# Memory keys and values as plain fp32 products, and a buffer of its own for the early weight tile of a stage

## The chip, the cores and the metric

The kernel runs on one core of a Trainium2 chip. The metric is the device time of one launch in microseconds (us), the median of several runs. Before the change three runs took 1684.59, 1685.55 and 1691.52 us.

## The reference

The program computes two transformer blocks of two layers each on a sequence of 256 tokens, width 1024, all in float32. Block 1 has a sliding-window attention with sinks and a sparse attention that keeps the 64 best keys of an index score; block 2 has a latent attention (MLA), a compressed/selected/window attention (NSA), a cross-attention to 256 memory tokens and a feed-forward net with a short convolution. The change touches the keys and values of the memory and the places where a weight tile is fetched early:

```python
memn = layer_norm_2(mem, ln_mem_g, ln_mem_b)                # once
for l in range(DEPTH):                                      # block 2, each layer
    ...                                                     # MLA and NSA, output projection, norm 1
    q = (x @ wq).reshape(B, S, XA_HEADS, XA_DH)             # XA_HEADS 4, XA_DH 256
    k, v = jnp.split(memn @ wkv, 2, axis=-1)                # wkv: 1024 x 2048
    s = jnp.einsum('bshd,bmhd->bhsm', q, k) * (XA_DH ** -0.5)
    o = jnp.einsum('bhsm,bmhd->bshd', jax.nn.softmax(s, -1), v)
    x = layer_norm_2(DEEPNORM_ALPHA * x + o @ wo, ln2_g, ln2_b)
```

`memn @ wkv` does not depend on the layers before it, so it can be computed at any time.

## The kernel before

Nearly every weight matrix comes as tiles of one megabyte (128 partitions x 2048 floats, line 653, issued by the sync engine SP). They land in a ring of five buffers, `raw`. Each is then split in two: ScalarE (ACT) writes the rounded high half `whi` (line 1171, three buffers), VectorE (DVE) subtracts it from the raw values to get the low half `wlo` (line 1498, five buffers). The activations are split in the same way (`xhi`, `xlo`; `memhi`, `memlo` for the memory). A product (`product`, lines 687 to 689) is then three matmuls in the fast reduced-precision fp32r format: high with high, high with low, low with high. `serve(key)` issues all splits whose high buffer is free once the tile of `key` is done on TensorE (PE); `hi_room` and `raw_room` give the tile that has to be done first. TensorE counts its finished tiles in `tile_done`.

Some products are plain fp32 matmuls on unsplit data: the attention scores and values, the compression weights `w1` (line 1063), and in the cross-attention the scores (line 1135) and values (line 1153). In the record of a run such a matmul leaves two entries: line 1135 runs 2 x 4 x 2 = 16 times a layer, 32 in all, and there are 64 entries.

The memory's keys and values of one layer of block 2 are eight tiles, `("kv", l, k)`. Four are worked off during each of the four attentions of the program (block 1 layers 0 and 1, block 2 layers 0 and 1). A tile is two halves (`memory_half`, line 766), each of 8 steps over the width, so 24 fp32r matmuls of 256 columns; there are 4 x 8 = 32 halves. `memory_slot` says at which attention step a half stands: steps 0 to 6 and 8 in block 1, steps 0, 2, 4, 6, 8, 10, 11 and 12 in block 2. ScalarE copies a half out (`memory_store`, line 1239) and sends it to memory.

An attention is a software pipeline over steps (a unit of a head kind and 128 tokens, in two halves of the heads). In step i TensorE does scores(i), a memory half, values(i-3), transposes(i-2). VectorE does the mask and the maximum of step i (line 1586), in block 1 also a piece of the top-k search (`top`), then the normalization of step i-1 (line 1620) and, behind some steps, a split. ScalarE does the exponentials of step i (line 1259), the copy of the memory half, and the copies of transposed probabilities (line 1282). Every engine works in the order in which its program was written.

Ahead of the attention in block 1, during the input projection, VectorE applies the rotary embedding (lines 1564 to 1569) and sums the index scores (line 1779) for token halves 0 and 1; the rectified scores that it sums come from ScalarE (line 1327) after TensorE (line 915).

Nine tiles are "extra" (`plan_extra`): the first tile of a stage behind an attention or a norm (`pg`, `xq`, `g` and `in`, each with index 0). They have no place in the ring. Their raw data land in the second half of `sy`, their halves in `ext`. The first half and second half of `sy` also hold the attention's probabilities (`soft`), so the load of `pg` 0 waits for the last values product of the attention (`pv_done`), that of `xq` 0 stands on SP behind the same wait, and that of `g` 0 in block 2 waits for the cross-attention (`xpT_ready`). In `split_order` an extra tile stands ahead of the ring tile it is tied to: `pg` 0 ahead of `o` 3, `xq` 0 ahead of `out` 3.

The output projection (`o` in block 1, `out` in block 2, four tiles) runs on TensorE in the order: tile 0 for both token halves, then tiles 1, 2, 3 for token half 0, then 1, 2, 3 for token half 1.

## Time and profile before

| | |
|---|---|
| median of three runs | 1685.55 us |
| the profiled execution | 1690.54 us, of which the recorded span is 1688.5 us |
| TensorE busy | 1534.9 us, 91% of the span |
| VectorE busy | 1097.6 us, 65% |
| ScalarE busy | 745.8 us, 44% |
| mean granted TensorE clock | 0.949 of full speed |
| the 217 low-half splits on VectorE | 489.6 us |
| the 217 high-half splits on ScalarE | 410.0 us |

The profile records one execution. PE is matmuls, DVE VectorE, ACT ScalarE, SP the sync engine that issues loads. An idle engine costs only where something waits for it. A matmul's recorded length is longer than its share of the array, since matmuls overlap in a pipeline: what one costs is read from start to start. The granted clock is a share of full speed, and its two levels are 2.4 GHz (1.0) and 1.2 GHz (0.5).

### The profile page before, as it was taken

What the parts mean: (1) busy time and instruction counts of PE and PEld (TensorE: products, weight loads), DVE (VectorE), ACT (ScalarE), POOL (GpSimd) and SP (SyncE); (2) the same over time, 40 slices, a digit from 0 to 9 for tenths busy, and PEclk for the clock granted to TensorE, in tenths of its full rate; (3) what the DMA queues carried; (4) which work ended last, traced back from release to release, by engine and by line L of the source; (5) the groups of instructions that cost most, each with busy time, mean ns of one, the idle gap of its engine ahead of it and who ended that gap; (6) DMA issues with size and microseconds to landing.
All of it is one profiled execution on the core that took longest, in us unless ns stands there. A gap on an engine that the chain in (4) does not pass through costs nothing.

```text
span 1688.5 us, 24734 instructions
## 1 busy us (share of the span) xinstructions
PE 1534.9 (91%) x10037; PEld 1380.7 (82%) x10037; DVE 1097.6 (65%) x1696; ACT 745.8 (44%) x1058; POOL 65.3 (4%) x58
## 2 busy tenths in 40 slices
PE   6788999999879999989888898999998888989997
PEld 5676899998767999968877778999788767789996
DVE  6886965467977754575464556677754745566766
ACT  4454433334553433334564334454445633344542
POOL 1200000000100000011000000000010000000000
PEclk9989999999899999989799999999997999989998
DMA  8523555655324655644424634556444246345551
GB/s 295 173 80 105 193 189 185 206 191 180 104 81 168 208 209 187 224 138 123 148 67 134 200 106 153 191 181 219 150 128 143 66 134 200 111 153 187 184 191 50
DMA packets 184692, 267.29 MB, mean 158 GB/s; under 512 B 7382, under 2 KB 139396, under 8 KB 184452
## 3 DMA queue, kind: packets, MB, share of 16 engines
q1 hardware_dynamic: 179684, 260.48, 46.6%
q10 hardware_dynamic: 4896, 5.25, 0.9%
q8 instruction: 80, 1.31, 0.3%
q14 instruction: 32, 0.26, 0.1%
HBM read 260.46 MB, written 5.24 MB: 157 GB/s over the span
## 4 chain that ended last, share of the span: by engine, by line
PE 66%; DVE 17%; DVEq 5%; ACT 4%; issue 3%; DMA 2%; POOL 2%; SPq 0%; ACTq 0%; POOLq 0%
PE psw L687 15%; PE psw L688 14%; PE psw L689 14%; PE psa L687 5%; PE psa L688 5%; PE psa L689 5%; DVE wlo L1498 4%; POOL rstd L2129 2%; DVE sy L1586 1%; DVE xtok L1530 1%; DVE r L1884 1%; PE psw L800 1%; DVEq L1590 1%; PE psa L822 1%; PE psw L1063 1%
## 5 line engine op out<-in xcount | busy, mean ns | idle before, releaser
L1498 DVE TENSOR_TENSOR wlo<-raw,whi 128x2048 fp32r<-128x2048 f32 (+2 forms) x217 | 489.6, 2262 | 299.3 <-ACT whi L1171 298.8
L1171 ACT ACTIVATE whi<-raw 128x2048 fp32r<-128x2048 f32 (+2 forms) x217 | 410.0, 1891 | 335.5 <-PE psw L689 243.4
L687 PE MATMUL psw<-xhi,whi 128*128 128x256 f32 x1472 | 416.8, 283 | 2.3 <-ACT r L1358 1.4
L688 PE MATMUL psw<-xlo,whi 128*128 128x256 f32 x1472 | 416.5, 283 | 0.0
L689 PE MATMUL psw<-xhi,wlo 128*128 128x256 f32 x1472 | 416.5, 283 | 0.0
L687 PEld LDWEIGHTS psw<-xhi,whi 128*128 128x128 f32 x1472 | 282.4, 192 | 4.7 <-ACT r L1358 2.2
L688 PEld LDWEIGHTS psw<-xlo,whi 128*128 128x128 f32 x1472 | 282.4, 192 | 1.2
L689 PEld LDWEIGHTS psw<-xhi,wlo 128*128 128x128 f32 x1472 | 282.5, 192 | 0.0
L687 PE MATMUL psw<-whi,xhi 128*128 128x512 f32 (+3 forms) x472 | 186.7, 396 | 28.6 <-DVE wlo L1498 26.1
L688 PE MATMUL psw<-wlo,xhi 128*128 128x512 f32 (+3 forms) x472 | 183.0, 388 | 0.0
L689 PE MATMUL psw<-whi,xlo 128*128 128x512 f32 (+3 forms) x472 | 182.2, 386 | 0.0
L687 PE MATMUL psa<-whi,rr 128*128 128x512 f32 x352 | 139.1, 395 | 5.4 <-DVE wlo L1498 5.4
L688 PE MATMUL psa<-wlo,rr 128*128 128x512 f32 x352 | 138.4, 393 | 0.0
L687 PEld LDWEIGHTS psw<-whi,xhi 128*128 128x128 f32 x472 | 91.3, 193 | 48.8 <-DVE wlo L1498 29.6
L689 PE MATMUL psa<-whi,rr 128*128 128x512 f32 x320 | 124.5, 389 | 0.0
L1471 ACT ACTIVATE r<-psw,pcol 128x256 f32<-128x256 f32 x88 | 45.0, 562 | 145.9 <-PE psw L689 145.9
L2084 DVE SCALAR_TENSOR_TENSOR r<-psw,pcol,r 128x255 f32<-128x255 f32 (+1 forms) x176 | 72.7, 475 | 54.2 <-ACT r L1471 52.6
L689 PEld LDWEIGHTS psw<-whi,xlo 128*128 128x128 f32 x472 | 91.5, 194 | 16.9
L688 PEld LDWEIGHTS psw<-wlo,xhi 128*128 128x128 f32 x472 | 91.5, 194 | 15.5
L2129 POOL TENSOR_TENSOR rstd<-vare,mhalf 128x1 f32<-128x1 f32 x26 | 39.6, 1524 | 1497.0 <-DVE vare L1520 1497.0
L1259 ACT ACTIVATE sy<-sy,nmx 128x256 f32<-128x256 f32 (+1 forms) x160 | 70.6, 444 | 45.9 <-DVE nmx L1599 45.9
L687 PEld LDWEIGHTS psa<-whi,rr 128*128 128x128 f32 x352 | 67.0, 190 | 19.2 <-issue 6.2
(270 smaller groups left out, 2147.0 us busy)
## 6 DMA issues: line engine op xcount, KB each, us to landing
raw<-in_w_gu SPq DMA_DIRECT2D x44, 1024.0 KB, 5.1
raw<-in_ffn_w_up SPq DMA_DIRECT2D x42, 1024.0 KB, 5.1
raw<-in_w_down SPq DMA_DIRECT2D x22, 1024.0 KB, 4.9
raw<-in_ffn_w_down SPq DMA_DIRECT2D x22, 1024.0 KB, 5.0
raw<-in_w_in SPq DMA_DIRECT2D x20, 1024.0 KB, 5.4
raw<-in_xa_wkv SPq DMA_DIRECT2D x16, 1024.0 KB, 5.7
raw<-in_w_o SPq DMA_DIRECT2D x8, 1024.0 KB, 5.1
raw<-in_w_out SPq DMA_DIRECT2D x8, 1024.0 KB, 5.1
```

The source lines that it names most:

```text
L687: pe.matmul(o, lh, rh, start=first, stop=False)
L688: pe.matmul(o, lh, rl, start=False, stop=False)
L689: return pe.matmul(o, ll, rh, start=False, stop=last)
L800: ins = pe.matmul(psw[:, 2 * (i % 2) + a, b * S:b * S + nk], qT(kind, h, t), kT(kind, h, nk), start=True, stop=True)
L822: ins = pe.matmul(psa[64 * b:64 * b + DH, 2, (h // 2) * P:(h // 2 + 1) * P], v(kind, h, kb), pt[:, m % 4, (q % 4) * P:(q % 4 + 1) * P], st ...
L1063: ins = pe.matmul(psw[:, i, 0:2 * NC], w1[:, j, :], cf[i][:, j, :, :].rearrange("p g n -> p (g n)"), start=(j == 0), stop=(j == 15))
L1171: nc.scalar.activation(tile_flat("hi", i), tile_flat("raw", i), ACT.Copy).then_inc(hi_ready, 1)
L1259: ins = nc.scalar.activation(soft[:, u % 2, h, 0:nk], soft[:, u % 2, h, 0:nk], ACT.Exp, bias=nmx[:, u % 2, h:h + 1], scale=1.0, accum_out= ...
L1471: ins = nc.scalar.activation(buf[:, f % 2, ch, :], bank2(psw, bank)[:, ch, :], ACT.Identity, scale=pcol[:, 2 + 2 * l, cc:cc + 1], bias=pco ...
L1498: v.tensor_tensor(tile_flat("lo", i), tile_flat("raw", i), tile_flat("hi", i).bitcast(F32), ALU.subtract).then_inc(lo_ready, 1)
L2084: ins = v.scalar_tensor_tensor(out=o, in0=bank2(psw, bank)[:, ch, 0:S - lag], scalar=pcol[:, j, cc:cc + 1], in1=o, op0=ALU.mult, op1=ALU.add)
L2129: g.tensor_tensor(rstd[:, t:t + 1], vare[:, t:t + 1], mhalf[:, t:t + 1], ALU.pow).then_inc(ln_rstd, 1)
```

## The change

The 16 `kv` tiles are no longer split: TensorE multiplies the raw tile with the unsplit transposed memory `memT`, one plain fp32 matmul a step in place of three fp32r ones. The 16 high-half and 16 low-half splits go, and the four low halves of the memory. A buffer of its own, `xraw`, takes the raw data of the extra tiles; their loads wait only until the previous extra tile is done. Outside the `in` stages an extra tile is now split behind its ring tile. The norm parameters ahead of `xq` are loaded two tiles later in SP's order. The wait for the stored memory halves moves with them.

```diff
-    halved = [i for i in ring if tiles[i][0][1] != "w1"]
+    halved = [i for i in ring if tiles[i][0][1] not in ("w1", "kv")]
@@
-        split_order += [e for e in extra if extra[e] == i] + [i]
+        here = [e for e in extra if extra[e] == i]
+        split_order += here + [i] if here and tiles[here[0]][0][1] == "in" else [i] + here
@@
-        memhi = sb("memhi", [KD, S], F32R)
-        memlo = sb("memlo", [KD, S], F32R)
+        memT = sb("memT", [KD, S])
+        xraw = sb("xraw", [2048])
@@
-                return {"raw": sy[:, 1, :], "lo": ext[:, 1, :], "hi": ext[:, 0, :]}[buf]
+                return {"raw": xraw[:], "lo": ext[:, 1, :], "hi": ext[:, 0, :]}[buf]
@@
-            gb_before[ti[(2, "xq", l, 0)]] = (2, "1", l)
+            gb_before[ti[(2, "xq", l, 2)]] = (2, "1", l)
@@
-                if key[1] == "xq" and key[3] == 0:
+                if key[1] == "xq" and key[3] == 2:
@@
-                if key[1] == "pg" and i in extra:
-                    sp.wait_ge(pv_done, 2 * (unit0(1, key[2]) + 4))
-                elif key[1] == "g" and i in extra:
-                    sp.wait_ge(xpT_ready, 4 * (key[2] + 1))
+                if i in extra and extra_use[i]:
+                    sp.wait_ge(tile_done, max(e for e in extra if e < i) + 1)
@@ memory_half
-                if half == 0:
-                    wh, wl = take(key)
-                else:
-                    wh, wl = tile_view("hi", ti[key]), tile_view("lo", ti[key])
+                pe.wait_ge(*loaded(ti[key]))
@@
-                        ins = product(psa[:, 3, 0:TC], wh[:, k, piece], wl[:, k, piece], memhi[:, k, :],
-                                      memlo[:, k, :], k == 0, k == KD - 1)
+                        ins = pe.matmul(psa[:, 3, 0:TC], weight[:, k, piece], memT[:, k, :],
+                                        start=k == 0, stop=k == KD - 1)
@@ ScalarE, input projection of block 1, layer 0
-                            turned_hi((2, "mem", 0), t, memhi)
+                            for b in range(2):
+                                act.wait_ge(mem_turned, 2 * t + b + 1)
+                                nc.scalar.activation(memT[:, 4 * b:4 * b + 4, t * P:(t + 1) * P], turned_bank(t, b),
+                                                     ACT.Copy).then_inc(mem_ready, 1)
@@ VectorE, the same place
-                    if l == 0 and q == 2:
-                        for t in range(NT):
-                            turned_lo((2, "mem", 0), t, memhi, memlo)
```

The order of VectorE's work ahead of the second layer's attention in block 1, before (`r` is its scratch, `sy` the rectified scores and temporaries):

```order
L1498 TENSOR_TENSOR wlo<-raw,whi 128x2048 [waits hi_ready] x2
L1564 TENSOR_TENSOR sy<-r,cos 128x576 [waits proj_ready]
...
L1498 TENSOR_TENSOR wlo<-raw,whi 128x2048 [waits hi_ready]
L1779 SCALAR_TENSOR_TENSOR r<-sy,wi_s,causal 128x128 [waits relu_done]
L1779 SCALAR_TENSOR_TENSOR r<-sy,wi_s,r 128x128 x7
L1564 TENSOR_TENSOR sy<-r,cos 128x640 [waits proj_ready]
...
L1498 TENSOR_TENSOR wlo<-raw,whi 128x2048 [waits hi_ready]
L1779 SCALAR_TENSOR_TENSOR r<-sy,wi_s,causal 128x256 [waits relu_done]
```

And now, on the same engine at the same place (line numbers are those of the changed kernel):

```order
L1499 TENSOR_TENSOR wlo<-raw,whi 128x2048 [waits hi_ready]
L1565 TENSOR_TENSOR sy<-r,cos 128x576 [waits proj_ready]
...
L1780 SCALAR_TENSOR_TENSOR r<-sy,wi_s,causal 128x128 [waits relu_done]
L1780 SCALAR_TENSOR_TENSOR r<-sy,wi_s,r 128x128 x7
L1565 TENSOR_TENSOR sy<-r,cos 128x640 [waits proj_ready]
...
L1780 SCALAR_TENSOR_TENSOR r<-sy,wi_s,causal 128x256 [waits relu_done]
```

Three splits are gone from between the rotary embedding and the index sums.

ScalarE at the end of the first attention of block 2, before: the extra tile `xq` 0 (`ext`) ahead of `out` 3 (the `whi` behind it), then `xq` 1.

```order
L1282 ACTIVATE pt<-psa 128x512 [waits pv_done,pt_done] x2
L1271 ACTIVATE xhi<-psa 128x4x128 [waits pv_done]
L1171 ACTIVATE ext<-sy 128x2048 [waits extra_loaded]
L1171 ACTIVATE whi<-raw 128x2048 [waits tile_done,tile_loaded2]
L1171 ACTIVATE whi<-raw 128x2048 [waits tile_done,tile_loaded3]
```

And now:

```order
L1280 ACTIVATE pt<-psa 128x512 [waits pv_done,pt_done] x2
L1269 ACTIVATE xhi<-psa 128x4x128 [waits pv_done]
L1169 ACTIVATE whi<-raw 128x2048 [waits tile_done,tile_loaded2]
L1169 ACTIVATE ext<-xraw 128x2048 [waits extra_loaded]
L1169 ACTIVATE whi<-raw 128x2048 [waits tile_done,tile_loaded3]
```

The split of `out` 3 has moved ahead of the extra one, which reads another buffer. VectorE's low halves moved in the same way.

SP at the same place, before (`gb` are the norm's parameters):

```order
L653 DMA raw<-in_w_out 128x4x512 [waits tile_done] x4
L615 DMA gb<-in_ln_g 128x1024 [waits kv_stored1,x_ready,kv_stored0,pv_done]
L616 DMA gb<-in_ln_b 128x1024
L653 DMA sy<-in_xa_wq 128x8x256
L653 DMA raw<-in_xa_wq 128x8x256 [waits tile_done] x3
```

And now:

```order
L654 DMA raw<-in_w_out 128x4x512 [waits tile_done] x4
L654 DMA xraw<-in_xa_wq 128x8x256 [waits tile_done]
L654 DMA raw<-in_xa_wq 128x8x256 [waits tile_done]
L618 DMA gb<-in_ln_g 128x1024 [waits kv_stored1,x_ready,kv_stored0,pv_done]
L619 DMA gb<-in_ln_b 128x1024
L654 DMA raw<-in_xa_wq 128x8x256 [waits tile_done] x2
```

The extra tile and `xq` 1 now stand ahead of the wait for the end of the attention.

## Rows read from the trace of the kernel before

**Rows 1.** The page: TensorE's busy line (part 1), the chain by engine (part 4).

```profile
PE 1534.9 (91%) x10037; PEld 1380.7 (82%) x10037; DVE 1097.6 (65%) x1696; ACT 745.8 (44%) x1058; POOL 65.3 (4%) x58
...
PE 66%; DVE 17%; DVEq 5%; ACT 4%; issue 3%; DMA 2%; POOL 2%; SPq 0%; ACTq 0%; POOLq 0%
```

**Rows 2.** Windows, first attention of each block: us, busy PE, PEld, DVE, ACT, POOL, clock.

```profile
90.00:148.00 58.00, 47.87 (x390) 41.96 (x390) 46.50 (x164) 33.10 (x96) 0.00 (x0) 0.90 0.22 73
...
842.00:907.00 65.00, 59.20 (x513) 51.24 (x511) 40.35 (x147) 42.95 (x129) 0.00 (x0) 0.95 0.20 66
```

**Rows 3.** Timeline of TensorE: start, length, instruction, what ended the idle time.

```profile
96.38 0.39 PE L687 MATMUL psa<-memhi,whi 128*128 128x256 f32 x1 [0.71 <-ACT r L1239]
...
99.37 1.13 PE L800 MATMUL psw<-r 64*128 64x256 f32 x8
...
969.90 7.17 PE L1135 MATMUL psw<-r 128*128 128x256 f32 x32 [0.69 <-ACT r L1446]
```

**Rows 4.** Groups by line and form, TensorE: the plain fp32 products of 256 columns.

```profile
L1135 PE MATMUL psw<-r 128*128 128x256 f32 x64 | 14.3, 382 | 1.4 <-ACT r L1446 1.4
```

**Rows 5.** The page, part 5: the group of low-half splits on VectorE.

```profile
L1498 DVE TENSOR_TENSOR wlo<-raw,whi 128x2048 fp32r<-128x2048 f32 (+2 forms) x217 | 489.6, 2262 | 299.3 <-ACT whi L1171 298.8
```

**Rows 6.** Timeline of all engines ahead of the second layer's attention, block 1.

```profile
421.73 2.29 DVE L1498 TENSOR_TENSOR wlo<-raw,whi 128x2048 fp32r<-128x2048 f32 x1 [0.37 <-ACT whi L1171]
...
432.33 1.15 PE L915 MATMUL psa<-r 32*128 32x256 f32 x16
...
432.82 2.29 DVE L1498 TENSOR_TENSOR wlo<-raw,whi 128x2048 fp32r<-128x2048 f32 x1
...
438.44 2.06 ACT L1327 ACTIVATE sy<-psa 128x512 f32<-128x512 f32 x4 [3.83 <-DVE r L1779]
...
440.96 2.29 DVE L1498 TENSOR_TENSOR wlo<-raw,whi 128x2048 fp32r<-128x2048 f32 x1
...
441.19 2.37 PE L907 MATMUL psw<-ident,r 128*128 128x128 f32 x10 [6.47 <-DVE r L1569]
...
443.16 0.48 DVE L1779 SCALAR_TENSOR_TENSOR r<-sy,wi_s,causal 128x256 f32<-128x256 f32 x1
```

**Rows 7.** Timeline in the first layer's attention, block 1.

```profile
95.81 0.29 DVE L1586 CUSTOM_DVE_ANT_0 sy<-psw,band 128x128 f32<-128x128 f32 x1
...
106.75 2.28 DVE L1498 TENSOR_TENSOR wlo<-raw,whi 128x2048 fp32r<-128x2048 f32 x1
...
113.59 0.35 PE L687 MATMUL psa<-memhi,whi 128*128 128x256 f32 x1 [3.45 <-ACT r L1239]
```

**Rows 8.** Windows view of TensorE alone, three stretches: its busy time, then granted clock.

```profile
86.00:95.00 9.00, 8.47 (x44) 0.54 0.01 3
...
864.00:869.00 5.00, 4.54 (x35) 0.67 0.01 3
...
922.57:928.00 5.43, 5.43 (x14) 0.58 0.00 0
```

**Rows 9.** Timeline in the first layer's attention, block 2.

```profile
857.01 2.28 DVE L1498 TENSOR_TENSOR wlo<-raw,whi 128x2048 fp32r<-128x2048 f32 x1
...
864.46 1.09 PE L822 MATMUL psa<-pt,r 128*64 128x128 f32 x16 [2.87 <-ACT pt L1282]
```

**Rows 10.** Timeline of the output projection of block 2, both layers.

```profile
907.03 0.50 PE L687 MATMUL psw<-whi,xhi 128*128 128x512 f32 x1
...
908.00 0.43 SPq L653 DMA_DIRECT2D sy<-in_xa_wq  x1
...
916.07 1.92 ACT L1171 ACTIVATE ext<-sy 128x2048 fp32r<-128x2048 f32 x1 [8.33 <-DMA sy<-in_xa_wq]
...
917.89 1.89 ACT L1171 ACTIVATE whi<-raw 128x2048 fp32r<-128x2048 f32 x1
...
922.57 0.79 PE L687 MATMUL psw<-whi,xhi 128*128 128x512 f32 x1 [4.37 <-DVE wlo L1498]
...
1385.30 0.79 PE L687 MATMUL psw<-whi,xhi 128*128 128x512 f32 x1 [5.47 <-DVE wlo L1498]
```

More of the change, by code:

```diff
@@ L325, in build @@
         extra_loaded = sem("extra_loaded")
+        mem_turned = sem("mem_turned")
+        mem_ready = sem("mem_ready")
         hi_ready = sem("hi_ready")
@@ L539, in build @@
         gb_before[ti[(1, "g", 1, 4)]] = (2, "in", 0)
-        turn_keys = [(1, "in", 0), (2, "mem", 0)]
+        turn_keys = [(1, "in", 0)]
         for l in range(L):
@@ L754, in norm_turns @@
                         ins = pe.transpose(turned_bank(t, b)[:, kk, :], src[:, t, k * P:(k + 1) * P], ident[:])
-                    ins.then_inc(act_turned, 1)
+                    ins.then_inc(mem_turned if key[1] == "mem" else act_turned, 1)
             def p_turns(l, bank):
@@ L769, in memory_half @@
                 key, half = (2, "kv", n // 16, n // 2 % 8), n % 2
-                if half == 0:
-                    wh, wl = take(key)
-                else:
-                    wh, wl = tile_view("hi", ti[key]), tile_view("lo", ti[key])
+                pe.wait_ge(*loaded(ti[key]))
                 if n:
                     pe.wait_ge(kv_staged, n)
-                piece = slice(half * P, (half + 1) * P)
+                weight, piece = tile_view("raw", ti[key]), slice(half * P, (half + 1) * P)
                 for k in range(KD):
                     if key[3] < 4:
-                        ins = product(psa[:, 3, 0:TC], wh[:, k, piece], wl[:, k, piece], memhi[:, k, :],
-                                      memlo[:, k, :], k == 0, k == KD - 1)
-                    else:
-                        ins = product(psa[:, 3, 0:TC], memhi[:, k, piece], memlo[:, k, piece], wh[:, k, :],
-                                      wl[:, k, :], k == 0, k == KD - 1)
+                        ins = pe.matmul(psa[:, 3, 0:TC], weight[:, k, piece], memT[:, k, :],
+                                        start=k == 0, stop=k == KD - 1)
+                    else:
+                        ins = pe.matmul(psa[:, 3, 0:TC], memT[:, k, piece], weight[:, k, :],
+                                        start=k == 0, stop=k == KD - 1)
                 ins.then_inc(tile_done if half else kv_part, 1)
@@ L929, in first_heads @@
                     if l == 0:
-                        pe.wait_ge(act_ready, 4 * (turn[(2, "mem", 0)] + 1))
+                        pe.wait_ge(mem_ready, 4)
                         pe.wait_ge(params_loaded, 16 * n_param_dmas)
@@ L1328, in rectified, with memory_out @@
                     ins.then_inc(relu_done, 1)
-                def memory_hi():
+                def memory_out():
                     if l == 0:
                         for t in range(NT):
-                            turned_hi((2, "mem", 0), t, memhi)
+                            for b in range(2):
+                                act.wait_ge(mem_turned, 2 * t + b + 1)
+                                nc.scalar.activation(memT[:, 4 * b:4 * b + 4, t * P:(t + 1) * P], turned_bank(t, b),
+                                                     ACT.Copy).then_inc(mem_ready, 1)
                 def first_heads_out():
@@ L1349, in _ @@
                 evict(1, "in", l, 7, 3, proj_out, {(1, 0): second_tokens},
-                      {(3, 1): memory_hi, (4, 1): first_heads_out, (5, 1): lambda: rectified(0)})
+                      {(3, 1): memory_out, (4, 1): first_heads_out, (5, 1): lambda: rectified(0)})
                 rectified(1)
```

## The prediction

> **What bounds the kernel now.** I read the page first: TensorE is busy for 91% of the span and the chain that ended last runs over it for 66%, over VectorE for 17% [rows 1]. So only two things can move the time: TensorE's own work, and the places where TensorE waits. The windows view of the attentions, where the memory halves lie, shows two different limits [rows 2]: in block 1 VectorE is busy 46.5 of 58 us and TensorE 47.9 with waits in between; in block 2 TensorE is busy 59.2 of 65 us. Then I read the timeline of the three places that the change touches: the way into the attention of block 1, the attentions, and the output projection behind them.
>
> **The product itself gets dearer.** A memory half before is 24 fp32r matmuls. From the start of one half to the start of what follows it is 99.37 - 96.38 = 2.99 us, 0.12 us a matmul and 0.36 for the three of a step [rows 3]. The nearest plain fp32 product of the same shape is the cross-attention's scores: its group has 64 entries for 32 products [rows 4], and one layer's 16 products last 7.17 us with the tail of the last, which is 0.44 us each from start to start [rows 3]. Eight steps are 3.55 us, so a half grows by 0.55 us, and 32 halves by 18 us of TensorE time. The bounds: nothing (the new products read a new buffer each, as the old ones did, so I exclude a gain below nothing by the start-to-start times), and 1.4 us a half, where a half meets the low clock (at half speed 0.88 a step against 0.72).
>
> The Trainium skill (FP8 and Floating Point Precision, section TensorE Precision Notes) says that a true fp32 product takes four passes through the array. At 2.4 GHz four passes of 256 columns would be 427 ns and three single passes 320, 27 us more over the 256 steps in place of my 18 to 21; that rule speaks against this half of the change, and the trace's 0.44 us agrees with it.
>
> **Into the attention of block 1.** Three of the four low-half splits of the kv tiles stand on VectorE around the rotary embedding and ahead of the index sums. A split is 2.26 us [rows 5]. In layer 1 the first also waited 0.37 us for its high half (it ended at 424.02) and the embedding behind it can start at 421.4, since what it reads was copied out before. The second (432.82) and third (440.96) follow [rows 6]. TensorE stood 6.47 us until 441.19 for the embedding that VectorE then finishes at 441.1 - 2.6 - 2.3 = 436.2 or earlier: it needs the last projection copy (432.8) and 2.6 us, so 435.4. The wait falls to under 1 us. The second index sum needs ScalarE's rectified scores, 2.06 us, which wait for TensorE's index scores, done at 432.33 + 1.15 = 433.5, and for the first sum. So it starts at 435.7 in place of 443.16: 7.5 us earlier [rows 6]. In layer 0 I take the same, though the four low halves of the memory go there too: TensorE's index scores limit it.
>
> **In the attention of block 1.** VectorE has no pause between its steps here, so its lead lasts if TensorE keeps up. The fourth split, at 106.75, goes as well: 2.3 us more, 9.7 in all [rows 7]. TensorE has to be through memory half 0 before scores(1). Up to now it ran there at the low clock, behind the long wait (0.54 from 86 to 95) [rows 8]. If the clock stays up, half 0 ends in time for VectorE's step 1, which was at 95.81 [rows 7]; if it falls as before, TensorE reaches step 1 only 4.9 us earlier and the sum is 4.9 + 2.3 = 7.2 us. The later halves are covered: TensorE waited 3.45 us ahead of the one at 113.59 for ScalarE, which waited for VectorE [rows 7], and eight halves cost 4.4 us more against the waits in this stretch, 58 - 47.9 = 10.1 us [rows 2]. I take the middle of 7.2 and 9.7, 8.3 us a layer after a little taken off for this: **16.6 us** less for two. If the cover fails entirely, the 4.4 us count fully and the gain is 3 us a layer.
>
> The Trainium skill (TensorE: Matmul & The Clock Gate, Part 1) ties the low clock to an array that was idle shortly before. The trace shows it here behind the 6.47 us and 4.37 us waits [rows 6, 8, 10]. By that rule alone the full 9.7 us would come, 19.4 for both layers.
>
> **In the attention of block 2.** Ahead of it TensorE is busy or waits for other things, so the two splits on VectorE there gain nothing. Inside, the first two halves are on the path: 0.8 us (half 0 is at the low clock) and 0.6, so TensorE's scores(3) come 1.4 us later. The split at 857.01, which goes, stood right ahead of the next mask [rows 9]: minus 2.3. TensorE's values product at 864.46 waited 2.87 us on that chain, which hides the third half; it comes 0.3 to 0.9 us earlier. The five halves behind it are mostly on the path, 0.55 each, about 2.5, and the low clock behind the wait (0.67 from 864 to 869) [rows 8] costs 5 x 0.33 = 1.6 us that may come back. Bounds: nothing, and all eight halves uncovered, 4.4 us. I take **1.5 us more** a layer, 3 in all.
>
> **The output projection.** Up to now the load of the extra tile is issued only when the attention has ended: 908.00, and lands at 916.07; ScalarE splits it, then `out` 3 at 917.89, and TensorE waits 4.37 us until 922.57; in layer 1 5.47 us until 1385.30 [rows 10]. Behind it TensorE runs 5.43 us at 0.58 of its clock [rows 8]: 5.43 x 0.42 = 2.3 us lost, and I take the same for layer 1. Now SP has issued the extra tile during the attention, and the split of `out` 3 stands first. What is late next is its high buffer: it is free when TensorE is through `out` 0, 907.03 plus 24 matmuls at 0.228 = 912.5. With 1.9 for ScalarE and 2.3 for VectorE it is ready at 916.8; TensorE comes to it behind 48 matmuls, at 918.0. So 1.2 us to spare, and the whole goes: 4.4 + 2.3 + 5.5 + 2.3 = **14.5 us** less. If it were late by 2 us, half of the wait and all of the low clock would stay, and 6 us remain as the gain. In block 1 the same split costs TensorE under 1 us; I leave it at nothing. The split of the extra tile now stands ahead of VectorE's first residual sum in the same way as before, and the norm's parameters are issued at the same moment, with less beside them. For `g` and `in` nothing waited on the load. The other early loads and the 16 ScalarE splits gain nothing else; ScalarE has slack (44%).
>
> **Sum.** -16.6 + 3 - 14.5 = -28.1 us. The profiled execution took 1690.54 us (2 us outside its span of 1688.5), 5.0 above the median of 1685.55. From its own time the sum gives 1662.4, and for the median of runs 1657.4.
>
> **Rivals.**
> - *TensorE becomes the bound in block 1's attention too.* For it: 47.9 of 58 us are busy already, and VectorE's lead is of use only if TensorE follows. Against: the wait of 3.45 us. Then VectorE's savings give nothing, the 32 halves cost 18 us in full, and only the output projection gains: +18 - 14.5, about 1689 for the median. I give it 0.08.
> - *Part of it:* the low clock at the entry to the attention remains, or `out` 3 is still late by a us or two. Then -14.4 + 4.4 - 8 = -18, 1668. This lies inside my forecast's own range; its outer part, 1672 to 1677, gets 0.08.
> - *Slower: the clock.* The new products keep TensorE at the low clock in the attentions of block 2. For it: plain fp32 stretches do stand beside low clocks (0.67 from 864 to 869, with transposes, scores and a half) [rows 8], and eight halves change from fp32r to fp32. Against: the window 842 to 907 has 0.95 as a mean [rows 2], with scores in fp32 throughout. It decides from the point where half of these 59 busy us are at 1.2 GHz: 30 us more in each of two layers, 60 in all, against the 28 gained: 1718. Chance 0.04.
> - *It does not do what it says:* the extra load is still issued late, because on SP it stands behind the last `out` load. That load waits for the second to last kv tile, which is done about 18 us before the end of the attention, so I give this 0.02, inside the second rival's time.
>
> **How the numbers follow.** The forecast, 1645 to 1672 for the median, has 0.78 (its lower end: 9.7 us twice, nothing lost in block 2, and half 0's clock, -19.4 + 0 - 15 = -34, and some for waits of the same kind that I have not priced). Its likeliest value is 1657. The other cases are the ones above: 0.08 up to 1677, 0.08 near 1689, 0.04 near 1718, and 0.02 below. Two runs of this kernel can be told apart at about 0.5%, 8.4 us: faster means under 1677. So faster 0.86 and a little for the unpriced, 0.87; same 0.08; slower 0.05. The range for 8 in 10 is 1644 to 1673.
>
> **What would show it.** In the new profile: entries of the new products (lines 777 and 780) with twice 0.22 us from start to start, a half of about 3.55 us; 201 low-half splits in place of 217; in block 1 no wait over 1.5 us ahead of the head transposes, a granted clock above 0.9 at the entry to the attention, and attentions that end 14 to 20 us earlier in sum; no wait of TensorE ahead of `out` 3, and a granted clock of 1.0 through the output projection; attentions of block 2 longer by up to 4 us. I am wrong if block 1's stretch to the end of the attention gains under 5 us a layer, if `out` 3 still waits, or if the halves take over 4.5 us.

## The result and the profile after

The changed kernel took 1657.51 us (median of four runs, 1655.66 to 1658.41) against 1687.01 us before in the same comparison: 0.9824 of the time, 95% interval 0.9802 to 0.9845, so 29.5 us less. The prediction said 1657.4, 28.1 us less. The two profiled executions lie further apart than the medians, 32.3 us in span.

The page of the changed kernel, busy times, chain by engine and the group of low-half splits:

```profile
PE 1539.2 (93%) x9781; PEld 1372.2 (83%) x9781; DVE 1055.2 (64%) x1676; ACT 716.3 (43%) x1042; POOL 62.9 (4%) x58
...
PE 71%; DVE 15%; ACT 4%; DVEq 3%; issue 3%; POOL 2%; DMA 1%; SPq 0%; ACTq 0%; POOLq 0%
...
L1499 DVE TENSOR_TENSOR wlo<-raw,whi 128x2048 fp32r<-128x2048 f32 (+2 forms) x201 | 452.7, 2258 | 327.4 <-ACT whi L1169 327.1
```

TensorE is busy 4.3 us more than before [rows 1], in a span 32.3 us shorter, so its waits shrank by 36.6 us. The 32 memory halves take 119.3 us of it in place of 108.7, summed from start to start; the rest of its work got shorter, at a mean clock of 0.959 in place of 0.949. The new products by line and form, and one half in the timeline of TensorE:

```profile
L780 PE MATMUL psa<-raw,memT 128*128 128x256 f32 x256 | 61.3, 394 | 1.5 <-ACT r L1237 1.4
L777 PE MATMUL psa<-memT,raw 128*128 128x256 f32 x256 | 60.6, 391 | 1.4 <-ACT r L1237 1.3
...
90.31 3.69 PE L777 MATMUL psa<-memT,raw 128*128 128x256 f32 x16 [0.67 <-ACT r L1237]
93.93 1.14 PE L798 MATMUL psw<-r 64*128 64x256 f32 x8
```

512 entries are 256 products. A half takes 93.93 - 90.31 = 3.62 us from start to start, 0.45 a step (the 28 halves that ran wholly at full clock took 3.46 to 3.65 us), as forecast from the cross-attention's scores [rows 4].

The way into the attentions of block 1 (timeline; then a window of TensorE, its busy time and granted clock):

```profile
82.12 1.42 PE L905 MATMUL psw<-ident,r 128*128 128x128 f32 x10 [0.94 <-DVE r L1570]
...
426.70 0.48 DVE L1780 SCALAR_TENSOR_TENSOR r<-sy,wi_s,causal 128x256 f32<-128x256 f32 x1
426.86 1.28 PE L905 MATMUL psw<-ident,r 128*128 128x128 f32 x10 [1.08 <-DVE r L1570]
```

```profile
86.00:90.00 4.00, 3.64 (x22) 1.00 0.00 2
```

The wait of 6.47 us in layer 1 [rows 6] is 1.08 now. In layer 0, where the clock stood at 0.54 before [rows 8], the wait is 0.94 and the clock is 1.00.

The output projection of block 2, layer 0 (ScalarE, VectorE, the first matmul of `out` 3 on TensorE; then a window of TensorE):

```profile
893.03 1.92 ACT L1169 ACTIVATE whi<-raw 128x2048 fp32r<-128x2048 f32 x1 [5.12 <-PE psw L690]
894.86 1.90 ACT L1169 ACTIVATE ext<-xraw 128x2048 fp32r<-128x2048 f32 x1
894.98 2.29 DVE L1499 TENSOR_TENSOR wlo<-raw,whi 128x2048 fp32r<-128x2048 f32 x1 [6.34 <-ACT whi L1169]
898.21 0.39 PE L688 MATMUL psw<-whi,xhi 128*128 128x512 f32 x1
```

```profile
893.00:898.00 5.00, 5.00 (x24) 1.00 0.67 210
```

`out` 3 is ready at 894.98 + 2.29 = 897.3 and TensorE comes to it at 898.2, behind 48 matmuls that began at 887.20: 0.9 us to spare, against the forecast's 1.2. The waits of 4.37 and 5.47 us [rows 10] are gone.

### Where the time went, stage by stage

TensorE's waits mark the same places of the program in every trace. I measured between them: block 1 from the wait at its first `in` tiles (7.7 us, in two traces 5.0) to the wait ahead of layer 1's `pg` 3; in block 2, for each layer, from the attention's first transposes to the cross-attention's. In the changed kernel these marks are

```profile
50.01 0.79 PE L688 MATMUL psw<-whi,xhi 128*128 128x512 f32 x1 [7.71 <-DVE wlo L1499]
516.27 0.50 PE L688 MATMUL psw<-whi,xhi 128*128 128x512 f32 x1 [1.55 <-DVE wlo L1499]
819.59 1.11 PE L1098 MATMUL psa<-ident,pt 128*128 128x128 f32 x4 [3.81 <-DVE pt L2043]
954.23 4.06 PE L1141 MATMUL psa<-ident,sy 128*128 128x128 f32 x16 [2.94 <-DVE sy L2067]
1279.00 1.11 PE L1098 MATMUL psa<-ident,pt 128*128 128x128 f32 x4 [3.81 <-DVE pt L2043]
1414.44 1.97 PE L1141 MATMUL psa<-ident,sy 128*128 128x128 f32 x8 [2.94 <-DVE sy L2067]
```

so block 1 takes 516.27 - 50.01 = 466.3 us and the two pieces of block 2 take 134.64 + 135.44 = 270.1. The rest is what else lies between the first mark and TensorE's last product. It is code that all kernels share (but for two experiments, marked *); some 50 us ahead of the first mark and 9 us behind the last product stand in no column. "Ratio" is to the kernel before on the same chip, with its 95% interval.

| kernel | ratio of the medians | block 1 | block 2, attentions to cross-attention | rest |
|---|---|---|---|---|
| before | 1 | 485.1 | 283.3 | 861 |
| changed | 0.9824 (0.9802 to 0.9845) | 466.3 | 270.1 | 861 |
| changed again | 0.9822 (0.9806 to 0.9838) | 465.4 | 270.5 | 859 |
| 1 buffer and orders alone | 0.9918 (0.9904 to 0.9933) | 484.2 | 270.4 | 859 |
| 2 plain products alone | 0.9904 (0.9891 to 0.9918) | 467.5 | 283.4 | 861 |
| 3 changed, old buffer | 0.9839 (0.9819 to 0.9860) | 465.8 | 272.3 | 866 |
| 4 changed, old split order | 0.9803 (0.9788 to 0.9818) | 465.4 | 270.5 | 859 |
| 5 both kv splits kept | 0.9941 (0.9929 to 0.9954) | 485.2 | 275.3 | 858 |
| 6 high splits kept | 0.9858 (0.9838 to 0.9877) | 471.4 | 268.8 | 860 |
| 7 low splits kept | 0.9970 (0.9959 to 0.9982) | 481.7 | 277.8 | 863 |
| 8 ten steps in block 1 | 0.9828 (0.9810 to 0.9846) | 469.2 | 271.4 | 861 |
| 9 ten steps in block 2 | 0.9876 (0.9857 to 0.9895) | 465.3 | 282.1 | 865 |
| 10 two tiles in norm waits | 0.9810 (0.9797 to 0.9824) | 466.2 | 271.0 | 860 * |
| 11 one tile in a norm wait | 0.9815 (0.9800 to 0.9830) | 465.8 | 269.3 | 861 * |

Where nothing differs, the first two columns of stages agree within 1.6 us, and the rest within 8 us. Much of that scatter is the clock (last section), and a difference of stages under 2 us, each from one trace, says little.

### The profile page after: what moved, and what is told of

It is laid out like the page before. It is cut to its first block, busy times and chain, and to the rows that moved or that the text cites. A ratio compares the mean times of both kernels' runs of the same rounds, so it can differ in the third digit from the quotient of the medians.

```text
span 1656.2 us, 24186 instructions
## 1 busy us (share of the span) xinstructions
PE 1539.2 (93%) x9781; PEld 1372.2 (83%) x9781; DVE 1055.2 (64%) x1676; ACT 716.3 (43%) x1042; POOL 62.9 (4%) x58
## 4 chain that ended last, share of the span: by engine, by line
PE 71%; DVE 15%; ACT 4%; DVEq 3%; issue 3%; POOL 2%; DMA 1%; SPq 0%; ACTq 0%; POOLq 0%
PE psw L688 16%; PE psw L690 16%; PE psw L689 16%; PE psa L688 4%; PE psa L689 4%; PE psa L690 4%; DVE wlo L1499 4%; POOL rstd L2127 2%; PE psa L780 2%; PE psa L777 2%; DVE xtok L1531 1%; PE psw L1061 1%; PE psw L798 1%; DVE r L1882 1%; DVE sy L1587 1%
## 5 line engine op out<-in xcount | busy, mean ns | idle before, releaser
L1499 DVE TENSOR_TENSOR wlo<-raw,whi 128x2048 fp32r<-128x2048 f32 (+2 forms) x201 | 452.7, 2258 | 327.4 <-ACT whi L1169 327.1
L1169 ACT ACTIVATE whi<-raw 128x2048 fp32r<-128x2048 f32 (+2 forms) x201 | 379.5, 1890 | 338.9 <-PE psw L690 247.4
L688 PE MATMUL psw<-whi,xhi 128*128 128x512 f32 (+3 forms) x472 | 184.9, 392 | 16.6 <-DVE wlo L1499 13.7
```

The lines of the kernel that those rows point to most:

```text
L688: pe.matmul(o, lh, rh, start=first, stop=False)
L1169: nc.scalar.activation(tile_flat("hi", i), tile_flat("raw", i), ACT.Copy).then_inc(hi_ready, 1)
L1499: v.tensor_tensor(tile_flat("lo", i), tile_flat("raw", i), tile_flat("hi", i).bitcast(F32), ALU.subtract).then_inc(lo_ready, 1)
```

## The experiments

### The two parts

**1, buffer and orders alone.** The kv tiles are split again and the memory is `memhi`, `memlo`; `xraw`, the split order and SP's order stay. (`xraw` has its room from `memlo`, so three of eight steps of the low halves are kept and used for all.)

```diff
-    halved = [i for i in ring if tiles[i][0][1] not in ("w1", "kv")]
+    halved = [i for i in ring if tiles[i][0][1] not in ("w1",)]
```

> The extra tile has its own buffer, the split order and SP's order are the new ones, but the kv tiles and the memory are split and multiplied in fp32r as before (of the memory's low halves only three of eight steps are kept, for want of space, and used for all). My theory: the two parts of the change add up, and this one gives the output projection alone, 15.2 us (6.8 and 8.4 us, from the two traces): 1687 - 15 = 1672 us, no wait of TensorE ahead of out 3, block 1 as before with its waits of 6 us ahead of the head transposes. Rival: the early loads are worth little unless VectorE is relieved too, because its kv splits stand behind the attention as well; then out 3 still waits some us and the time is 1678 or more.

**2, plain products alone.**

```diff
-                return {"raw": xraw[:], "lo": ext[:, 1, :], "hi": ext[:, 0, :]}[buf]
+                return {"raw": sy[:, 1, :], "lo": ext[:, 1, :], "hi": ext[:, 0, :]}[buf]
-        here = [e for e in extra if extra[e] == i]
-        split_order += here + [i] if here and tiles[here[0]][0][1] == "in" else [i] + here
+        split_order += [e for e in extra if extra[e] == i] + [i]
```

> The kv tiles and the memory are unsplit and multiplied in plain fp32, but the extra tile keeps its old buffer, split order and place on SP. My theory: this part alone gives what lies in the attentions and ahead of them, 29.5 - 15 = 14 us of the median: 1673 us, TensorE's waits of 4.4 and 5.5 us ahead of out 3 unchanged. Rival: the product's price of 18 us is hidden only because the other part of the change makes room; then this one alone is at 1680 or above.

Measured: 1675.59 and 1673.26 us beside 1689.51 before, so 13.9 and 16.3 us less. The sum, 30.2, agrees with the 29.5 of the whole within the intervals of some 2.5 us. Each keeps exactly its own waits. TensorE in 1, ahead of the head transposes:

```profile
87.67 0.66 PE L909 MATMUL psw<-ident,r 128*128 128x128 f32 x2 [6.02 <-DVE r L1571]
441.84 2.37 PE L909 MATMUL psw<-ident,r 128*128 128x128 f32 x10 [6.47 <-DVE r L1571]
```

and in 2, ahead of `out` 3:

```profile
906.24 0.50 PE L689 MATMUL psw<-whi,xhi 128*128 128x512 f32 x1 [4.39 <-DVE wlo L1500]
1368.30 0.79 PE L689 MATMUL psw<-whi,xhi 128*128 128x512 f32 x1 [5.49 <-DVE wlo L1500]
```

The parts add up, and neither rival holds.

### Inside the second part: buffer or order

**3, the old buffer with the new order** (`sy`, and SP's waits as before).

> As the changed kernel, but the extra tile lands in sy as before, so its load is issued when the attention has ended; the split order is the new one (out 3 ahead of the extra tile). My theory: the order does most of the work, since out 3 needs only its high buffer, and xq 0 itself isn't needed until TensorE has done the norm's transposes, more than 15 us later. Its low split would come about 1 us into VectorE's first residual sum. So 1 us a layer is lost against the changed kernel: 1659 to 1661 us, no wait ahead of out 3. Rival: the buffer does it; then this kernel has the waits of 4.4 and 5.5 us and stands at 1672.

**4, the new buffer with the old order** (the one line of `split_order` as in 2).

> As the changed kernel with its buffer and early load, but with the old split order (the extra tile ahead of out 3). My theory: the tile has landed when ScalarE comes to it, it is split while ScalarE would wait for the high buffer of out 3 anyway, and nothing is lost: 1657 to 1658 us, no wait ahead of out 3. So either half of this part does it alone. Rival: the split of the extra tile pushes that of out 3 back by 1.9 us on ScalarE and 2.3 on VectorE, over the 1.2 us to spare; then 3 us a wait and the low clock behind it, 5 us a layer: 1667.

Measured: 3 at 1663.51 us (range 1656.85 to 1665.50) and 4 at 1656.67, beside 1689.51. Neither has a wait ahead of `out` 3. In 3 the extra tile comes late, as said (ScalarE, then VectorE, whose first residual sum stands behind it):

```profile
898.75 1.92 ACT L1171 ACTIVATE ext<-sy 128x2048 fp32r<-128x2048 f32 x1 [1.14 <-DMA sy<-in_xa_wq]
...
900.70 2.29 DVE L1501 TENSOR_TENSOR ext<-sy,ext 128x2048 fp32r<-128x2048 f32 x1 [0.77 <-ACT ext L1171]
902.91 0.68 DVE L1641 SCALAR_TENSOR_TENSOR xtok<-xtok,psw 128x512 f32<-128x512 f32 x1
```

That costs 2.0 us in the two pieces (272.3 against 270.3), the 1 us a layer of the expectation. By the ratios 3 is 2.7 us behind the changed kernel, with intervals of some 3 us each way; the longer rest of its profile (866) lies where the kernels are alike. In 4 the extra tile is split in ScalarE's pause:

```profile
888.98 1.91 ACT L1168 ACTIVATE ext<-xraw 128x2048 fp32r<-128x2048 f32 x1
894.20 1.92 ACT L1168 ACTIVATE whi<-raw 128x2048 fp32r<-128x2048 f32 x1 [3.31 <-PE psw L689]
```

So either half does most of it alone: what hurt before was a split that waited for a late load and stood ahead of `out` 3. Reordering alone gives some 11 of the 13 us, and the buffer with its early load gives all of it.

### What the kv splits cost, engine by engine

**5, both splits kept:** plain products, but ScalarE and VectorE still split the kv tiles for nobody.

```diff
+    halved = [i for i in ring if tiles[i][0][1] not in ("w1",)]
...
+                v.tensor_tensor(tile_flat("hi" if tiles[i][0][1] == "kv" else "lo", i), tile_flat("raw", i), tile_flat("hi", i).bitcast(F32),
...
+                if half == 0:
+                    take(key)
```

> As the changed kernel, with plain products on the raw kv tiles, but ScalarE and VectorE still split these 16 tiles (the halves are written and not read) and TensorE still waits for them; only the memory itself stays unsplit. My theory: what block 1 gained came from VectorE's time, and so it all goes back: 18.7 us there (wait of about 6 us ahead of the head transposes, attention's step at VectorE's pace), and 2.8 us in each attention of block 2 where a split stood ahead of the mask: 1657.5 + 18.7 + 5.6 = 1682 us. The dearer products stay hidden in block 1 behind the waits that come back. Rival: block 1's gain came from something else (TensorE's clock in the halves, the memory's four low halves): then 1660 to 1668 us.

Measured: 1680.23 us. Block 1 is back at 485.2, to 0.1 us where it was before the change. TensorE ahead of the head transposes of layer 1, and in block 2's first attention:

```profile
441.53 2.37 PE L906 MATMUL psw<-ident,r 128*128 128x128 f32 x10 [6.47 <-DVE r L1571]
...
866.44 1.97 PE L821 MATMUL psa<-pt,r 128*64 128x128 f32 x16 [2.77 <-ACT pt L1281]
```

Though its halves are 0.6 us longer than before, block 1 is no slower: with the splits kept, the products' price there is hidden, to within the 1 us or so by which such stages scatter. The memory itself is unsplit here, and in sum with the dearer products that comes out at nothing, so its four low halves were no visible part of the gain.

**6, only ScalarE's high halves kept, and 7, only VectorE's** (a subtraction of the raw tile from itself; the other engine's split is skipped):

```diff
+                if tiles[i][0][1] == "kv":
+                    return
```

> As the changed kernel, but ScalarE still makes the high halves of the 16 kv tiles (not read by anyone), and TensorE waits for them; VectorE's low halves are gone. It parts the relief of ScalarE from that of VectorE. My theory: VectorE is what bound block 1, ScalarE had room, and this costs at most 3 us against the changed kernel (16 x 1.9 us of ScalarE time, nearly all of it beside other work). Rival: ScalarE's copies (the memory half, the transposed probabilities) stand behind its split in the attention's chain as much as VectorE's mask behind the low split: then 8 us or more of the 21 to 24 us of the kernel with both splits.

> The other part: VectorE still does one subtraction of the size of the low split for each of the 16 kv tiles (of the raw tile from itself, into a buffer that nobody reads), and TensorE waits for it, while ScalarE has no kv splits. My theory: nearly all of what the kernel with both splits lost comes back, 18 to 22 us more than the changed kernel, a wait of about 5 to 6 us ahead of the head transposes in block 1. Rival: under 12 us, since the low split no longer waits for ScalarE's high half and slides into VectorE's gaps.

Measured: 6 at 1664.76 and 7 at 1684.28 us, beside 1658.46 for the changed kernel on the same chip: 6.3 and 25.8 us more. In the stages of block 1 it is 5.6 us for ScalarE's splits (471.4 against 465.8, the mean of the two changed runs), 15.9 for VectorE's and 19.4 for both. TensorE in 7:

```profile
437.41 2.36 PE L907 MATMUL psw<-ident,r 128*128 128x128 f32 x10 [5.97 <-DVE r L1580]
```

In layer 0 it waits 3.66 us there. VectorE was the bound, as stated. But ScalarE's splits, four of 1.9 us a layer, gave more than the 3 us that I expected of both blocks, though the engine is busy only 43% of the time. (The ratios, with some 4 us each way, don't part 6.3 us from the rival's 8; the 5.6 us of the stage do better.) In 6 VectorE's wait ahead of the head transposes is as short as in the changed kernel (1.09 us in layer 1), and yet the memory half behind them takes 5.34 and 5.95 us in the two layers, not 3.65. ScalarE ahead of it in layer 1, in 6 and then in the changed kernel, and the window of TensorE in each:

```profile
425.81 1.91 ACT L1171 ACTIVATE whi<-raw 128x2048 fp32r<-128x2048 f32 x1
427.62 2.05 ACT L1327 ACTIVATE sy<-psa 128x512 f32<-128x512 f32 x4
...
431.00:440.00 9.00, 7.90 (x35) 0.62 0.00 1
```

```profile
424.60 2.06 ACT L1325 ACTIVATE sy<-psa 128x512 f32<-128x512 f32 x4 [0.72 <-PE psa L913]
...
428.00:437.00 9.00, 7.18 (x44) 1.00 0.05 17
```

In the changed kernel ScalarE waits for the index scores; in 6 the split stands ahead of them, and they come out 1 us later. TensorE waits 0.68 us longer for the head copies behind them, and then runs at a clock of 0.62 in place of 1.00. In layer 0 it is the same (0.81 us more, and the half at 0.68 of the clock). From the head transposes to the last values these attentions take 59.5 and 60.5 us, against 57.4 in both traces of the changed kernel (clock 0.97 and 1.00). The low clock is not wholly owed to the splits: in nine kernels without kv splits, two layers each, the first half met it once (2, layer 1, 0.74), in 6 in both layers.

6 against 5 also says what VectorE's relief is worth while ScalarE still splits: 485.2 - 471.4 = 13.8 us in block 1. The 5.6 us are what ScalarE's adds to it.

7 is slower than 5, which keeps more splits: 25.8 us behind the changed kernel against some 20 by the ratios. By the stages the two are nearly alike (23.4 and 24.4 us in sum), and 5 us of the difference lie in their rest (863 and 858). In block 2 7 loses 7.5 us and 5 only 5.0. From the third memory half of layer 1 to the fourth 7 takes 13.7 us and 5 takes 11.4; why, no run here shows. The subtraction needn't wait for a high half in 7, and stands at another moment.

### Is TensorE's time covered?

**8 and 9: ten steps in place of eight, in block 1 or in block 2** (steps 0 and 1 are added twice).

```diff
-                for k in range(KD):
+                steps = list(range(KD)) + ([0, 1] if n // 16 == 0 else [])
+                for q, k in enumerate(steps):
```

> As the changed kernel, but each memory half in the attentions of block 1 has ten steps in place of eight (steps 0 and 1 are added twice), 2 x 0.44 us more for 16 halves: 14.1 us of TensorE time in all. It asks whether TensorE's time is covered there. In the changed kernel TensorE still waits 5.1 and 6.3 us in these attentions, of it 1.6 us at their ends, where no half can use it. My theory: the two engines are close to balance, the first 1 to 3.5 us a layer are covered and the rest is on the path: 7 to 12 us more, 1665 to 1669 us. Rival: VectorE sets the pace and covers it: under 3 us more. The other: TensorE sets it, all 14 us come, 1672.

> The same in block 2 alone: 16 halves with ten steps there, 14.1 us more TensorE time. TensorE waits only 2.7 and 2.1 us in these attentions now. My theory: TensorE sets the pace, 12 to 14 us more, 1670 to 1672 us, and nothing of block 1 changes. Then the product's price of 0.6 us a half was on the path in block 2 too, and what hid it in the result was the 2.8 us wait that went with the split. Rival: there is cover that the waits don't show (TensorE's products overlap with what it would wait for): under 7 us more.

Measured: 1662.49 and 1667.94 us beside 1689.73. Of 14.1 us of added TensorE time, 3.4 come through in block 1 (469.2) and 11.8 in block 2 (282.1). By the ratios it is 0.8 and 9 us, with intervals of some 3 us each way. So in block 1 it is the rival that is near, not my 7 to 12 us, and in block 2 somewhat less than the 12 to 14 us of the theory. Windows of block 1's two attentions in 8, all engines (us, busy PE, PEld, DVE, ACT, POOL, clock), then of the first attention in the two traces of the changed kernel:

```profile
82.00:142.00 60.00, 56.63 (x373) 45.47 (x373) 45.87 (x164) 34.90 (x100) 0.00 (x0) 1.00 0.32 107
430.00:490.00 60.00, 57.58 (x376) 46.41 (x377) 45.40 (x163) 33.66 (x97) 0.00 (x0) 1.00 0.33 106
```

```profile
82.00:139.50 57.50, 50.92 (x330) 40.14 (x330) 45.60 (x166) 34.88 (x102) 0.00 (x0) 0.97 0.36 120
...
81.40:138.80 57.40, 49.38 (x330) 38.95 (x330) 45.61 (x166) 34.74 (x101) 0.00 (x0) 1.00 0.35 119
```

The waits fill with work: from the head transposes to the last values these attentions take 59.5 and 59.3 us, against 57.4 with eight steps, so some 2 of the 7 us added to each come through. With eight steps it is 57.4 us at a clock of 0.97 and at 1.00 alike, as where another engine sets the pace. In block 2 there is little to fill. So the price of the plain products (0.6 us a half) was mostly hidden in block 1 and mostly real in block 2.

### Into the waits that are left

**10, two kv tiles out of block 2's first attention into TensorE's waits of 5.2 us for the norms; 11, one tile, into the second of them.**

```diff
+SLOTS2_0 = (0, 4, 8, 11)
...
+                if l == 0:
+                    memory_half(20, 2)
+                    memory_half(21)
                 norm_turns((2, "1", l), 1)
...
+                if l == 0:
+                    memory_half(22, 2)
+                    memory_half(23)
                 norm_turns((2, "2", l), 1)
```

> A version for the better, from the waits that are left: behind the output projections of block 2's first layer TensorE waits 5.2 us for VectorE's norm, twice. Four of the memory halves (two tiles) move from the attention of block 2, layer 0, to these two places, two to each, with a small buffer for what ScalarE copies out. My theory: the attention gets shorter by up to 4 x 3.6 = 14.4 us, since TensorE is its bound, less 1 to 3 us where VectorE and ScalarE then set the pace; each pair takes about 7.4 us in place of a wait of 5.2, so 4.4 us come back; the clock may stay up behind them. In sum 7 to 10 us less than the changed kernel: 1647 to 1650 us. Rival: the attention falls to the pace of VectorE's and ScalarE's chain and gives under 6 us: then 1656 or no gain. The other: the two halves delay the copies that the norm's second transposes need; then they are late by more than 2 us each and it is 1657 or above.

> Only one tile (two memory halves) moves out of the attention of block 2, layer 0, into TensorE's wait of 5.2 us for the norm behind xo; six halves stay in the attention. In the kernel with two tiles moved the attention took 66.7 us from its first transposes to its last values, as with all eight halves, with waits of 1.5 to 2.5 us and the clock at 0.90, and only the place behind xo gave 2.1 us. My theory: with six halves the attention is between the two limits and gives 1 to 3 us, and the norm's wait 2 us: 3 to 5 us less than the changed kernel. Rival: the attention's length is set by VectorE's and ScalarE's chain as well, and stays at 66.6: then 2 us or less, which can't be told from no gain.

Measured: 1657.72 us beside 1689.73 (0.9810), and 1658.26 beside 1658.46 for the changed kernel. The rival in which the chain over VectorE and ScalarE sets the length holds in both, and neither theory's gain (7 to 10 us, 3 to 5 us) is there. With 14 us of TensorE work taken out, the attention of 10 is as long as before: from its first transposes to its last values 66.65 us, against 66.58 and 67.06 in the two traces of the changed kernel. TensorE's waits in it, and its window beside that of the changed kernel:

```profile
836.01 0.66 PE L833 MATMUL psa<-pt,r 128*64 128x128 f32 x8 [1.83 <-ACT pt L1306]
...
869.19 0.66 PE L833 MATMUL psa<-pt,r 128*64 128x128 f32 x8 [2.17 <-ACT pt L1306]
883.84 1.09 PE L833 MATMUL psa<-pt,r 128*64 128x128 f32 x16 [2.46 <-ACT pt L1306]
```

```profile
822.00:888.00 66.00, 54.25 (x381) 43.12 (x382) 38.63 (x146) 40.49 (x125) 0.00 (x0) 0.89 0.18 57
```

```profile
822.00:887.00 65.00, 62.30 (x450) 50.45 (x449) 38.07 (x146) 41.04 (x128) 0.00 (x0) 0.98 0.30 98
```

TensorE waits for the chain over VectorE and ScalarE instead, and its clock sinks from 0.98 to 0.89: for the 14 us of work taken out its busy time falls by 8 only (62.30 to 54.25). Adding work here costs most of it (9), taking work away gives nothing. The two limits lie at about the same length. No version beat the changed kernel by what can be measured. 4 is the lowest, and its interval overlaps.

## Why the prediction was right

The median came out within 0.1 us of the number said. That closeness is luck: the terms were off by up to 5 us, in both directions, and so was the start (1685.55 then, 1687.01 in the comparison). What held is the mechanism, term by term:

- **Products, +18 us of TensorE time in 32 halves.** Right: 3.62 us a half at full clock against the 3.55 forecast. (The upper bound given for a half at the low clock, 1.4 us, is 1.3 by its own figures, 8 steps of 0.88 - 0.72.)
- **Block 1, -16.6.** The attentions ended 7.8 and 9.0 us earlier, 16.8 in sum. The wait at the entry shrank as worked out: the second index sum of layer 1 starts at 426.70 against 443.16, of which 9.0 is layer 0's gain, so 7.5 us earlier, the forecast's number. The clock stayed up, and the product's price was mostly covered (5, 8). One term was missing, though: the forecast put all of this down to VectorE and said that the ScalarE splits "gain nothing else". With ScalarE's splits kept, VectorE's relief gives 13.8 us in block 1, and ScalarE's the other 5.6 (5, 6). The forecast's lower branch, 7.2 us a layer with the low clock left at the first half, is near what VectorE's relief alone gives (the attentions end 6.2 and 7.6 us earlier in 6 than in 5, with the first half at low clock in both layers). So the term of 16.6 us had the wrong make-up, and it came near the 16.8 by luck: too much put down to VectorE, nothing to ScalarE. Between the marks block 1 gained 18.8 us: the other 2 came in its output projections, where the forecast left the extra tile's split at nothing. TensorE waited 0.91 us for it in layer 0 and 0.41 in layer 1; in experiment 1 these waits are gone without the plain products, and in 2, with the old order, 0.39 and 0.36 us are left.
- **Block 2's attentions, +3.** Measured -0.2 and +0.45 us. Windows of TensorE from one memory half to the next, before (the third half's step, then those of the sixth and the seventh):

```profile
856.26:868.33 12.07, 9.20 (x82) 0.89 0.07 22
...
885.88:891.55 5.67, 5.67 (x50) 1.00 0.19 59
891.55:897.31 5.76, 5.76 (x59) 1.00 0.43 160
```

and the same steps of the changed kernel:

```profile
836.68:845.92 9.24, 8.68 (x75) 1.00 0.17 62
...
864.09:870.42 6.33, 6.33 (x43) 1.00 0.20 44
870.42:876.91 6.49, 6.49 (x50) 1.00 0.89 321
```

The late steps cost 0.7 us each, against the forecast's 0.55, and 0.3 where a wait was left. But the step with the removed split gave 2.83 us (12.07 - 9.24), the wait and the low clock behind it, where I had taken 2.3 and only said that the clock "may come back"; and the first two halves cost nothing (6.93 us before and 6.94 now, 7.61 and 7.53), where I had set 1.4.
- **Output projection, -14.5.** From the end of the attention to the norm's wait: 29.20 us in both layers against 35.98 and 37.56, so 6.8 + 8.4 = 15.1. Right by its own steps, with 0.9 us to spare for the 1.2 forecast. The reason was right too, but more than needed: the order alone or the buffer alone would have done (3, 4). What the forecast missed is behind it: from the norm's wait to the cross-attention's mark TensorE takes 38.9 and 39.3 us now against 38.0 and 38.5, at a mean clock of 0.89 against 0.92. 1, 3 and 4 show the same (38.6 to 39.4 us), and 2, with neither the order nor the buffer, does not (38.0 and 38.5). So some 0.8 us a layer is given back, and the two pieces of block 2 gain 13.2 us.
- **The rest** was forecast at nothing, and is so within its scatter.

A plain product's step took 0.45 us. The Trainium skill (FP8 and Floating Point Precision, section TensorE Precision Notes) counts four passes for a true fp32 product, which by estimate are 0.43 us for 256 columns at 2.4 GHz; the trace agrees within 0.02 us.

The rivals fell for named reasons: TensorE did not become the bound in block 1 (8: 3.4 of 14.1 us come through), the clock in block 2's first attention did not sink but rose (0.95 [rows 2] to 0.98), and the extra load was issued in time (its split follows that of `out` 3 with no wait, at 894.86).

## What to carry to other kernels

Price a cheaper or dearer product by the stage that it stands in. The same dearer product was nearly free where another engine set the pace and cost its full 0.6 to 0.7 us where TensorE did, and eight 1.9 us splits of an engine that was idle more than half of the time still cost 5.6 us, since they stood ahead of a copy that was due. When a stage's limits have met, as in block 2's attention, work taken from one engine alone buys nothing.

A split or copy that waits for a late load holds up everything in its engine's program behind it: put the item that is needed first ahead of it, or let the load start earlier. One of the two is enough, and the order costs no memory.

## What the runs showed of the hardware

The low clock begins at different moments of the same code. In the stage between the last FFN and block 2's second attention, windows of TensorE before and in the changed kernel (us, busy, clock), both reckoned from the same wait of 0.41 us, at 1280.30 and 1255.38:

```profile
1283.00:1285.00 2.00, 2.00 (x20) 1.00 0.03 8
1285.00:1287.00 2.00, 2.00 (x14) 0.64 0.74 205
```

```profile
1256.00:1258.00 2.00, 2.00 (x18) 0.86 0.97 341
1258.00:1260.00 2.00, 2.00 (x12) 0.50 0.01 4
```

Before, the clock falls some 5.3 us behind that wait, now 2.1 us, and the stage takes 99.9 us in place of 97.0. The changed kernel was run again to see whether this is a matter of the kernel or of the execution, and the stage took 99.4 us, with the clock falling 2.7 us behind the wait: near enough to the first that it decides nothing. Over all kernels here the stage took 97.0 us before and in 2 and 6, 97.3 in 7, 98.1 in 5, and 99.3 to 99.9 in the other nine. 6 has the changed kernel's code in this stage, so the code of the stage alone does not fix it; whether the earlier changes play a part stays open. Executions of one kernel do differ: in the two traces of the changed kernel it is 93.8 and 95.2 us from block 2's first norm to its first attention, and 224.8 and 222.6 us in the stage with the first FFN behind it. The Trainium skill (TensorE: Matmul & The Clock Gate, Part 1) says that the monitor runs on a time of its own that doesn't start with the kernel, so that the same kernel changes its clock at other points from run to run; the two traces of the changed kernel agree with that. For reading a result it means that some us between two profiles of this program are nothing (the rest column, the same code throughout, runs from 858 to 866 us), and a stage between two marks tells more than the span.

The clock also answers to the work: in block 2's first attention it is 0.98 in both traces of the changed kernel, with eight memory halves, 0.95 with six (11) and 0.89 with four (10), though none of TensorE's waits in that window of 10 is over 2.5 us. In block 1's attentions no such thing can be told: with eight steps it is 0.97 in one trace of the changed kernel and 1.00 in the other, with ten steps 1.00. Behind the norm's first wait of 5.2 us TensorE runs at 0.50 in the changed kernel, and at 1.00 where two memory halves fill the wait (10):

```profile
915.40:921.00 5.60, 4.95 (x22) 0.50 0.98 290
```

```profile
919.00:925.00 6.00, 4.77 (x35) 1.00 1.07 386
```
